# Block 2 of a two-block model on one core: positions modulo sixteen, values in two float16 halves, other queues for the loads

## The reference

```
# block 1: layer norm, input projection, three mixers (spatial gating, convolution of 31 taps,
#          attention in a band of +-128 keys with 8 query heads and 2 key heads), projection, residual, layer norm
# block 2:
h = rmsnorm(x, g);  z = h @ w_in                      # 1024 -> 4096
q, k = rope(q, pos), rope(k, pos)                     # 12 heads of 64
for window, d in ((128, 1), (512, 4), (2048, 16)):    # position s sees s, s-d, s-2d, ... down to s-128d
    o_i, lse_i = softmax attention on positions regrouped by s mod d
o = sum_i softmax(lse)_i * o_i;  attn = o * silu(g_attn)
conv = c_b * causal_conv3(c_c * c_h) * silu(g_conv)
x = x + rmsnorm([attn, conv] @ w_out, g_post)
```

## Time and profile before

| | us |
|---|---|
| median of 3 runs | 2588.72 (2577.92 to 2594.11) |
| the profiled execution | 2575.78 |
| its span, first to last instruction | 2573.9 |
| PE busy | 2346.1 (91%) |
| DVE busy | 1406.4 (55%) |
| ACT busy | 843.0 (33%) |
| POOL busy | 686.1 (27%) |

### The profile page before, as it was taken

The page is one execution under the profiler, slowest core; times in us unless marked ns, Lnnn a source line. Parts: engine busy times, 40 slices in busy tenths (PEclk is TensorE's granted clock), DMA queues, the critical chain, the costliest instruction groups (busy, mean ns, idle before and its releaser), DMA issues.

```text
span 2573.9 us, 47860 instructions
## 1 busy us (share of the span) xinstructions
PE 2346.1 (91%) x18958; PEld 2138.0 (83%) x18958; DVE 1406.4 (55%) x3441; ACT 843.0 (33%) x1938; POOL 686.1 (27%) x654
## 2 busy tenths in 40 slices
PE   6999899797788899699999999999798999897898
PEld 5978799797688788689888889899698899896777
DVE  6514768945698444663465632121576677675322
ACT  4411111111677100442122201011576677565111
POOL 0012021144231898101111121210114443543222
PEclk9999899898899899899999999999899999998999
DMA  4341320124851322423555522111957876864442
GB/s 151 107 113 51 95 88 17 50 92 149 199 129 36 130 102 99 160 89 102 177 174 177 163 76 70 46 66 46 228 142 183 208 185 175 198 188 151 154 137 105
DMA packets 283824, 322.19 MB, mean 125 GB/s; under 512 B 38112, under 2 KB 221280, under 8 KB 280144
## 3 DMA queue, kind: packets, MB, share of 16 engines
q1 hardware_dynamic: 281776, 313.09, 42.1%
q0 software_dynamic: 1680, 5.51, 0.7%
q10 hardware_dynamic: 144, 0.52, 0.0%
HBM read 196.91 MB, written 109.56 MB: 119 GB/s over the span
## 4 chain that ended last, share of the span: by engine, by line
PE 68%; DVE 9%; DMA 8%; issue 6%; SPq 3%; POOL 3%; ACT 2%; DVEq 0%; POOLq 0%; ACTq 0%
PE bank L163 52%; DMA cm<-scr_part 4%; PE bank L1783 4%; PE bank L1812 3%; DVE acc L642 3%; PE bank L1784 3%; PE bank L1794 3%; SPq L1903 1%; PE bank L352 1%; POOL yo L2061 1%; DMA qTB<-scr_qh 1%; POOL Y L1143 0%; DMA woR<-in_w_out 0%; PE bank L1217 0%; PE bank L1049 0%
## 5 line engine op out<-in xcount | busy, mean ns | idle before, releaser
L163 PE MATMUL bank<-w1h,xh 128*128 128x256 f32 (+1 forms) x896 | 260.3, 291 | 14.9 <-DVE s1st L632 14.9
L163 PE MATMUL bank<-w1l,xh 128*128 128x256 f32 (+1 forms) x896 | 256.3, 286 | 0.0
L163 PE MATMUL bank<-w1h,xl 128*128 128x256 f32 (+1 forms) x896 | 256.0, 286 | 0.0
L163 PE MATMUL bank<-xh,w2h 128*128 128x512 f32 x640 | 249.0, 389 | 0.0
L163 PE MATMUL bank<-xl,w2h 128*128 128x512 f32 x640 | 249.0, 389 | 0.0
L163 PE MATMUL bank<-xh,w2l 128*128 128x512 f32 x640 | 249.0, 389 | 0.0
L163 PE MATMUL bank<-w2h,xh 128*128 128x256 f32 x768 | 219.6, 286 | 9.9 <-issue 6.6
L1849 DVE CUSTOM_DVE_ANT_0 s2m<-bank,mask 128x256 f32<-128x256 f32 (+1 forms) x576 | 186.6, 362 | 67.6 <-PE bank L1784 63.9
L163 PE MATMUL bank<-w2l,xh 128*128 128x256 f32 x768 | 219.0, 285 | 0.0
L163 PE MATMUL bank<-w2h,xl 128*128 128x256 f32 x768 | 218.9, 285 | 0.0
L642 DVE SCALAR_TENSOR_TENSOR acc<-ain,cw,acc 128x512 f32<-128x512 f32 x240 | 200.1, 835 | 8.9 <-ACT acc L599 1.8
(11 more groups left out here) (258 smaller groups left out, 6203.4 us busy)
## 6 DMA issues: line engine op xcount, KB each, us to landing
v<-scr_v SPq DMA_DIRECT2D x12, 1552.0 KB, 9.1
scr_part<-ob SPq DMA_DIRECT2D x48, 264.0 KB, 3.2
cm<-scr_part SPq DMA_DIRECT2D x48, 264.0 KB, 5.3
w2r<-in_w_in SPq DMA_DIRECT2D x12, 1024.0 KB, 6.2
qr<-qf SPq DMA_DIRECT2D x192, 64.0 KB, 2.1
scr_v<-bvo SPq DMA_DIRECT2D x24, 388.0 KB, 2.5
v<-scr_v SPq DMA_DIRECT2D x24, 388.0 KB, 5.7
ax<-in_x SPq DMA_DIRECT2D x16, 512.0 KB, 5.9
```

The costliest lines, as they stand in the source:

```text
L163: ins = nc.tensor.matmul(dst, x, y, start=k == 0 and m == 0, stop=k == n - 1 and m == 2)
```

## The change

1. x1 is written with its rows ordered by position modulo sixteen (row r·128 + l holds position 16·l + r), and block 2 works in this order throughout; the output's rows are put back by the last store. Rope reads cosine and sine through a view of step 16; the convolution of three taps uses whole blocks of 128 columns as shifts. Values are written twice: v23 in the new order and v21 in the old.
2. Values have two float16 parts, scaled by a bound that is computed on the chip from the weights (DVE, and a sum over partitions on POOL). The product with the values has three matmuls in place of five, in `window_stage` too; VW is 130.
3. In `dilated_stage` blocks of queries and keys are runs of 8·d positions. For d < 16 POOL copies the queries of four units in one piece beforehand ("reorder"); with d = 16 a block is contiguous. PE makes the scores of two units together, in two banks. Scores go straight to p2r, which has six buffers; s2m is gone.
4. The patterns come as 16, 4, 1 (the last pair 1, 4, 16). Masks for d = 4 and 1 are loaded behind the first pair's operands in 20 DMAs and rearranged by DVE at step 8.
5. Queries and keys of later pairs are loaded from POOL's queue. Values come in four DMAs a pattern, at steps 7, 9, 11 and 13. A quarter's partial results come in eight DMAs in place of two, and B starts eleven steps behind A.

```diff
-VW = 194
+STRIPES = {1: 16, 4: 4, 16: 1}
+VW = 130
...
-vo = sbs(f"{tag}vo", 2, [128, vt, vh, 194 if ones else 192], BF, scope)
+vo = sbs(f"{tag}vo", 2, [128, vt, vh, VW if ones else 128], FH, scope)
...
-                elif x_ready is not None:
-                    sp.wait_ge(*x_ready[t])
+                elif t == 0:
+                    for token in x_ready:
+                        sp.wait_ge(*token)
...
+                            act.wait_ge(*d_vs.at(3 * valued.index(n) + 3))
+                            nc.scalar.activation(value_part(o, 0), value_view(bank), ACT.Identity, scale=fit[:, n:n + 1]).then_inc(*a_v.up())
...
+        def dve_bound(n):
+            nc.vector.tensor_reduce(wmax[:, n, :], wts.raw[:, :, cols], mybir.AxisListType.X, ALU.max, apply_absolute_value=True).then_inc(*d_bd.up())
...
+        def pool_bound(n):
+            nc.gpsimd.partition_all_reduce(bound[:, n, 1:2], bound[:, n, 0:1], 128, bass.bass_isa.ReduceOp.add).then_inc(*g_bd.up())
...
-                for m, (a, part) in enumerate(((ph, 0), (ph, 1), (ph, 2), (pl, 0), (pl, 1))):
+                for m, (a, part) in enumerate(((ph, 0), (ph, 1), (pl, 0))):
...
-            nc.scalar.dma_start(x1[128 * (NT - 1):S, :], xr[(NT - 1) % 5][:]).then_inc(*x_last.up(16))
+            nc.scalar.dma_start(x1_rows(NT - 1), xr[(NT - 1) % 5][:]).then_inc(*x_last.up(16))
...
-        return [(x_out[t], x_out[t].base + 16) for t in range(4)]
+        return [s.now() for s in (*x_out, x_last)]
...
+                cos, sin = (b[:].rearrange("p (l r) -> p r l", r=16)[:, 4 * x["g"]:4 * x["g"] + 4, :] for b in (cosT, sinT))
...
-            mixing.append([t, [None] * delay + ["A"] + [None] * (3 if j < 5 else 0) + list("BCDEFG")])
+            mixing.append([t, [None] * delay + ["A"] + [None] * (10 if j < 5 else 0) + list("BCDEFG")])
...
-                        mix(j, quarter, quarter == 3, 9 * quarter, "pool", work)
+                        mix(j, quarter, quarter == 3, 2 + 8 * quarter, "pool", work)
...
-            if g == 6 and n + 1 < len(pairs):
-                work.append(("values", n + 1))
+            if g in (7, 9, 11, 13) and n + 1 < len(pairs):
+                work.append(("values", n + 1, g // 2 - 3))
+            if s == 8:
+                work.append(("mask copies",))
+            if s % 2 == 0 and s - s % 4 + 8 in fours:
+                work.append(("reorder", s - s % 4 + 8, s % 4 // 2))
...
-            if item[0] == "scores":
+            if item[0] == "scores" and item[1] % 2 == 0:
+                two = units[item[1]:item[1] + 2]
...
-                qc, kc = slice(q0, q0 + d * 127 + 1, d), slice(k0, k0 + d * (w - 1) + 1, d)
+                            q = buf[hh][:, 128 * g:128 * g + 128] if d == 16 else qd[x["of4"] % 3][hh][:, g % 4, :]
+                            keys = buf[(4 if second else 2) + hh]
+                            ins = nc.tensor.matmul(dst, q, blocks(keys[:], d)[:, k0:g + 1], start=not second, stop=second)
...
-                        for m, (a, v_at, n) in enumerate(((ph, 0, 65), (ph, 66, 64), (ph, 130, 64), (pl, 66, 64), (pl, 0, 65))):
+                        for m, (a, v_at, n) in enumerate(((ph, 0, 65), (ph, 66, 64), (pl, 0, 65))):
...
+            elif item[0] == "reorder":
+                if n >= 3:
+                    pool.wait_ge(*p_s.at(fours[n - 3] + 4))
+                nc.gpsimd.tensor_copy(qd[n % 3][hh][:].rearrange("p t (r l) -> p t r l", l=8 * d), blocks(qk[j % 2][hh][:], d)[:, g:g + 4]).then_inc(*g_q.up())
...
-                for n in range(2):
-                    nc.sync.dma_start(cm[slot][:, :, n, :], part[n][j][rows, :].rearrange("(t p) c -> p t c", p=128)).then_inc(*cm_in[slot].up(16))
+                for n, d in enumerate((4, 1)):
+                    for i in range(4):
+                        t = 4 * q + i
+                        src = part[d][j].rearrange("(r b s l) c -> r s b l c", r=d, b=NT // d, s=STRIPES[d])[t % d, t // d]
+                        nc.sync.dma_start(cm[slot][:, i, n, :], src).then_inc(*cm_in[slot].up(16))
```

328 lines of the change are left out of this document (204 added, 124 removed).

## The result

The changed kernel is not faster. The median of 20 runs is 2596.5 us (2589.9 to 2607.4) against 2586.0 (2569.8 to 2595.6) in 20 runs of the kernel before on the same chips: a ratio of 1.0042, 95% interval 1.0027 to 1.0057. That is 0.4% slower, within the 1% that the forecast calls the same, and 102 us above the forecast.

The account below looks back on a forecast made before the run. PE was taken as the bound, with DMA waits beside it, and DVE after the change. Dilated stage −102, other terms +8 +2 −3 +1: −94 on 2575.8 gives 2482, scaled to 2494 us; eight in ten 2455 to 2555.

Parts of the forecast that it names:

- Product with the values, scores: Dilated stage, PE: fewer value matmuls save 9.1 us a pair, contiguous queries in the scores 16.6 us a pair.
- Rival B: Dilated stage: moving operand in short runs costs what strided rows cost; 74 us a pair, 2536 us in all; chance 0.13.
- DVE as the bound: Dilated stage: DVE's 62.1 us a pair bounds, 65 at 95% busy; 67 with 2 us added, 88 us won over four pairs.
- DMA: Dilated stage: 64 us of DMA in a 65 us pair, nearly full but not one queue; most of 11 us waiting goes.
- rival C: Dilated stage: POOL's short-run copies become the bound; slower from 2.3 us a copy, 2665 us at 3.3; chance 0.05.
- Pair 0: Dilated stage's first pair: d = 16 takes 38 us behind mask loads, the pair 83 in place of 87.8; 5 us won.
- Pair 5: Dilated stage's last pair, with mixing on DVE within the last pattern: 74 us in place of 83; 9 us won.
- Between the blocks: Start of block 2: all 16 stores of x1 must land before the first load; 8 us lost.
- Window stage: Block 1's window stage: PE loses 23 us of work but DVE is nearly full; 3 us won, bounds 0 to 6.
- Rope, bound: Rope's strided reads, at most twice as long, hidden: nothing; the values' bound and scale: 1 us each for stages a and b.
- Rival D: Earlier stages lose more: rope's DVE up to 20 us, sum over partitions up to 19; 2525 us; chance 0.12.
- rivals A: Dilated stage: engines fit together better, 62 to 64 us a pair; 2468 us in all; chance 0.25.

Follow-up runs that it names:

- a1: Changed kernel with most loads of queries and keys (pairs 2 to 5) and of partial results (from third quarter) left out, three kept-row buffers: 2499.4 us, 67.9 a pair.
- d3: c2 with the loads of d = 4's partial results by tile again, as in the change: 2569.3 us, 85.8 a pair.
- e3: Changed kernel with most loads of queries and keys of pairs 2 to 5 left out (64 columns for 2048): 2529.9 us, 74.2 a pair.
- e6: Changed kernel with the next pair's ten query and key loads every third step in place of every second: 2596.7 us, 91.5 a pair.
- d1: c2 with the next pair's queries and keys loaded at steps 20 to 38 in place of 8 to 26: 2569.6 us, 84.8 a pair.
- d4: c2 with two buffers for the kept rows of d = 16 in place of three: 2548.6 us, 81.2 a pair.
- c1: Changed kernel with d = 4's partial-result loads by runs of 32 partitions, three kept-row buffers and masks from ACT's queue: 2543.3 us, ratio 0.984.
- c2: c1 with the stores of partial results also issued from ACT's queue: 2531.2 us, ratio 0.9802, 76.5 a pair.
- f1: c2 with the next pair's queries and keys loaded from SP's queue again: 2561.0 us, 83.5 a pair.
- f2: c2 with mixing step B four steps behind A, as before the change, in place of eleven: 2531.4 us, 80.8 a pair.
- d2: c2 with the mixing list advancing four quarters at a time, not two, in the last pattern: 2525.9 us, ratio 0.9777.
- w1: Changed kernel with five product matmuls per block of keys again in block 1's window stage: stage 163.4 us, whole 2616.1 us.
- e8: Changed kernel with the 20 mask loads issued from ACT's queue at the start of the stage: 2589.0 us, pair 0 75.6 us.
- e4: Changed kernel with most loads of partial results left out from the third quarter on (8 rows for 128): 2562.2 us, 84.9 a pair.

## Why the prediction was wrong, by its steps

- **Product with the values, scores: right.** 0.36 us and 0.58 us a unit against 0.37 and 0.56. Rival B is out, with the moving operand in runs of eight floats.
- **DVE as the bound: right where nothing waits.** 20.3 to 21.7 us a pattern with DVE at 98 to 99%; and a pair of 67.9 us in the kernel with the loads all but gone, for a forecast of 67. The sign "PE near 80%" did not come: PE was busy 94 to 100% of the three undisturbed patterns, 57.3 us together where the forecast had 52.4.
- **DMA: this step failed.** It read "Most of the 11 us of waiting goes". Instead DVE's waits for `cm`, for the stores of `ob` and for the kept rows grew from 12.5 to 19 us a pair, and d = 4 took 40.2 us against 25.8 in the kernel with the loads all but gone (a1). I had counted bytes (64 us of DMA in 65) and the time from load to use, and nothing of the form of the eight new loads, though I named their number. Loads of four runs use four engines, by the events of their semaphores, and cost 38 us in all, by d3.
- **Nearly full is full.** "Nearly full, but no longer in one queue" took 64 of 65 us as enough room. The pair's loads cost 15 us a pair (e3) even so, and moving them in time only moves the place (e6, d1). Shares of this kind have to be asked by window: before, the share was already 1.03 in the one pattern that mixes.
- **A wait was missed.** The eleven steps between A and B end the mixing of quarter 3 so late that the next pair but one waits for its kept rows: 17 us by d4. The working followed the new delay forwards to what it relaxes, not to who frees a buffer at its end.
- **SP's queue.** The forecast said nothing of the stores behind the eight loads; 12 us, from c1 to c2.
- **POOL: right and harmless.** 0.60 us a copy where 0.8 was taken; rival C, that POOL becomes the bound, is out. A copy would have had to take 2.3 us. The loads on its queue, which the forecast held for nearly neutral, win 30 us (f1).
- **Pair 0: right.** 81.9 us for 83, its first pattern 39.8 for 38; the other profiles of the same code have 85.7 to 87.4 and 43.4 to 44.9.
- **Pair 5: wrong by 7 us**, 81.4 for 74; and behind it 12 us more until the first output transposes, where I had 1. POOL's mixing lies there. Earlier mixing shortens this part (f2, d2) but lengthens pair 5 by 7 and 16 us, so little is won in all.
- **Between the blocks: right in kind, 4 us short.** +12 for +8. The forecast took the store's 2.6 us from a contiguous one; the reordered one took 6.0, which is the 3.4 us that were missing. Its semaphore's nine events for sixteen are the same sign as the five of the loads above. Its shape was not tried alone.
- **Window stage: 14 us won for 3**, outside the bounds of 0 to 6. DVE at 75.6 of 80 us leaves 5.5% of 171 us, 9 us, to win; 14 were won, as DVE's own busy time fell by 7.6 us too, 4.5 of it because it met POOL's subtractions less, which was luck (w1). 6 us are the matmuls, which is the forecast's upper bound.
- **Rope, bound: right.** 1.47 us for 1.11 is less than the doubling that I costed, hidden. The sum over partitions takes 0.4 to 0.7 us. Rival D is out.

The rivals A, B, C and D all spoke of engines. None said that the DMA engines and the queue order take back the whole gain, though the forecast itself had put the DMA engines at 64 of 65. C was the one case that ended slower, and it is out; the gain was lost in another way. The single prices: shape 38, kept rows 17, stores 12 and masks 9 (by e8, one execution) are 76 us, and 2596.5 minus 2531.2 is 65; the edits overlap.

## What to carry to other kernels

When a change makes the engines faster and leaves the traffic, work out the DMA engines' share in each stretch after the change, not over a period, and look at the form of each new load: one tile from a few separate runs uses few of the engines, the share over a whole pattern can still read 0.87, and the load holds every store behind it in the same queue. The number of events in which a load's semaphore rises tells it. When a step is put later, look for the buffers that it frees, as far as two periods ahead. And where a gain doesn't appear, a kernel with the loads made tiny shows at one blow whether the engines' side of the reasoning was right.

## What the runs showed of the hardware

- A load of 66 KB whose rows come in four runs of 32 rows, over 128 partitions, raised its semaphore in five events, one at the end of the issue and four as data landed; as 32 partitions with four rows each in sixteen. While such loads were what DVE waited for, the DMA share was 0.28 for 5 us (1944.5 to 1949.5 of the changed kernel). A store of 512 KB whose rows go out as 8 × 16 had nine events and took 6.0 us to land, a contiguous one sixteen and 2.6.
- An issuing engine stands still when such loads are behind: single issues of up to 4.7 us for them and 5.9 for the load that follows them, against at most 1.5 with the other shape; eight loads took SP up to 15.7 us whole, and 2.7 to 4.7 with 8 of their 128 rows (e4).
- A strided read of 64 bytes a step costs DVE 0.36 us on 512 columns (medians 0.69 to 1.05 us and 0.68 to 1.04), half as much again and not a doubling.
- While POOL subtracts, a DVE instruction that starts can take until POOL's ends: 2.34 us for 0.16 in the window stage before (three times), 4.1 to 5.5 for 1.05 in the rope stage after (six times of 96).
- POOL copies 512 columns in runs of eight floats in 0.60 us, and sums a column over the partitions in 0.4 to 0.7.
- PE's granted clock was 0.80 over the stalled 42.2 us and 1.00 in the patterns where PE had no long gaps: the same d = 4 units show 25.4 us of busy PE there and 19.5 where PE ran on. Right behind the stop the clock was 0.50 and twelve products took 0.67 us, at 1.00 they took 0.36: a wait is thus dearer than its own length.
